# Issuing the expert-row gathers four and four in turn, in place of eight and eight

## The reference

```
for a chunk of 128 tokens, for each of 8 heads:
    s1, i1 = top 16 of the first 128 scores;  s2, i2 = top 16 of the second 128
    cand   = all 256 sums s1 + s2;            top_s, top_c = top 16 of cand
    idx    = 16 expert numbers per token (out of 16384);  gate = softmax(top_s)
    act[k]  = gelu( dot(u_tbl[idx[k]], x) )             k = 0..15
    out    += sum over k of gate[k] * act[k] * v_tbl[idx[k]]
```

## Time and profile before

| | |
|---|---|
| median of 3 runs | 1637.37 us (1636.74 to 1637.39) |
| the profiled execution | 1637.88 us, of which the span is 1636.1 us |
| busy in the span | PE 85%, DVE 61%, POOL 59%, ACT 23% |
| chain that ended last | PE 44%, DMA 26%, issue 10%, DVE 10%, POOL 5%, ACT 4% |
| DMA | 613.88 MB, 375 GB/s over the span; gathers 536.94 MB of it |

### The profile page before, as it was taken

One profiled execution on the slowest core, in us unless ns is written; L12 is line 12 of the kernel. 1 busy time (PEld: TensorE's weight loads), 2 busy tenths in 40 slices (PEclk: granted clock), 3 DMA queues, 4 the chain that ended last, 5 costly groups with the idle time before them and its releaser, 6 DMA issues.

```text
span 1636.1 us, 17816 instructions
## 1 busy us (share of the span) xinstructions
PE 1389.7 (85%) x4977; PEld 802.9 (49%) x4977; DVE 991.3 (61%) x2405; ACT 373.7 (23%) x903; POOL 972.8 (59%) x1038
## 2 busy tenths in 40 slices
PE   7999888887777989876989798986998887888886
PEld 6987454543333554533556455553554553333332
DVE  2147726557677636556656665557774667666664
ACT  1012212212222123322221312232322322222221
POOL 0026545657777655655674755566676477777773
PEclk9999999998998989987999999998999998888887
DMA  9639989999999999999999999999999899999997
GB/s 325 202 115 400 347 309 364 366 363 379 410 410 409 402 394 394 387 395 401 409 404 362 398 394 394 394 396 408 389 409 401 324 410 409 410 409 410 410 409 289
DMA packets 220137, 613.88 MB, mean 375 GB/s; under 512 B 17636, under 2 KB 87332, under 8 KB 220068
## 3 DMA queue, kind: packets, MB, share of 16 engines
q0 software_dynamic: 147456, 536.94, 84.1%
q1 hardware_dynamic: 72468, 75.54, 13.6%
q10 hardware_dynamic: 144, 0.52, 0.1%
HBM read 611.88 MB, written 1.05 MB: 375 GB/s over the span
## 4 chain that ended last, share of the span: by engine, by line
PE 44%; DMA 26%; issue 10%; DVE 10%; POOL 5%; ACT 4%; POOLq 0%; ACTq 0%; DVEq 0%
PE sums L553 28%; DMA rows<-in_peer_u,expert 22%; PE banks L500 11%; DVE rows L1080 4%; POOL rows L455 4%; PE banks L507 2%; POOL rows L467 2%; DMA wring<-in_attn_w_q 2%; DMA wring<-in_w_kv 2%; ACT diag L820 1%; PE sums L507 1%; PE banks L539 1%; ACT L812 1%; DMA rows<-in_peer_v,expert 1%; DVE coef L1098 1%
## 5 line engine op out<-in xcount | busy, mean ns | idle before, releaser
L553 PE MATMUL sums<-rows,diag 128*128 128x512 f32 x2032 | 975.1, 642 | 202.9 <-ACT diag L820 200.1
L1080 DVE SCALAR_TENSOR_TENSOR rows<-rows,xn_near 128x1024 f32<-128x1024 f32 x512 | 616.0, 1220 | 315.5 <-DMA rows<-in_peer_u,expert 305.0
L553 PEld LDWEIGHTS sums<-rows,diag 128*128 128x128 f32 x2032 | 414.2, 207 | 738.9 <-issue 580.6
L467 POOL DMA_INDIRECT rows<-in_peer_v,expert x512 | 483.6, 945 | 342.6 <-PE sums L553 247.9
L455 POOL DMA_INDIRECT rows<-in_peer_u,expert x512 | 487.1, 951 | 299.2 <-issue 249.7
L500 PE MATMUL banks<-xT,wring 128*128 128x128 f32 (+1 forms) x1536 | 210.6, 297 | 7.2 <-DMA wring<-in_attn_w_q 3.3
L500 PEld LDWEIGHTS banks<-xT,wring 128*128 128x128 f32 x1536 | 199.5, 195 | 23.5 <-issue 10.6
L820 ACT ACTIVATE diag<-ident,coef 128x128 f32<-128x128 f32 x508 | 155.5, 388 | 32.0 <-DVE coef L1098 31.8
L812 ACT ACTIVATE gelu<-dots 128x8 f32<-128x8 f32 (+1 forms) x65 | 13.4, 207 | 429.8 <-DVE rows L1080 429.7
L1098 DVE SCALAR_TENSOR_TENSOR coef<-gelu,gate_inv,gate 128x8 f32<-128x8 f32 (+1 forms) x65 | 14.9, 229 | 89.6 <-ACT gelu L812 88.5
L761 ACT ACTIVATE soft<-banks 128x256 f32<-128x256 f32 (+1 forms) x27 | 11.4, 422 | 243.9 <-PE banks L500 243.9
(11 more groups left out here) (115 smaller groups left out, 733.9 us busy)
## 6 DMA issues: line engine op xcount, KB each, us to landing
wring<-in_peer_w_query SPq DMA_DIRECT2D x23, 1024.0 KB, 16.6
wring<-in_w_kv SPq DMA_DIRECT2D x16, 1024.0 KB, 26.0
rows<-in_peer_u,expert POOLq DMA_INDIRECT x512, 10.4
rows<-in_peer_v,expert POOLq DMA_INDIRECT x512, 10.6
wring<-in_attn_w_q SPq DMA_DIRECT2D x8, 1024.0 KB, 23.3
rows<-in_conv_w_in SPq DMA_DIRECT2D x7, 1024.0 KB, 12.0
wring<-in_conv_w_in SPq DMA_DIRECT2D x5, 1024.0 KB, 11.1
wkept<-in_conv_w_out SPq DMA_DIRECT2D x4, 1024.0 KB, 12.0
```

The costliest lines, as they stand in the source:

```text
L467: pool.indirect_dma_start(v_row[j], None, v_table, bass.IndirectOffsetOnAxis(ap=expert[b][:, k:k + 1], axis=0)).then_inc(v_landed[j], 16)
L553: last = nc.tensor.matmul(sums[:, half, :], diag[:, k % GROUP, :], v_row[k % V_SLOTS][:, half * 512:(half + 1) * 512], start=(first and k ...
L1080: nc.vector.scalar_tensor_tensor(out=u_row[j], in0=u_row[j], scalar=1.0, in1=xn_near[:, :, :].rearrange("p a d -> p (a d)"), op0=ALU.mult, ...
```

## The change

For each group the loop over u and the loop over v become two functions, and they are called for the first four places of u, the first four of v, the last four of u and the last four of v. No wait, no semaphore count, no gather and no place changes; only the order in which GpSimd goes through them does. The waits move with their gathers. The other engines' programs stay as they are.

```diff
+            def gather_u(n, b, g, js):
+                for j in js:
+                    if not (isinstance(n, int) and n == 0 and g == 0):
+                        pool.wait_ge(dot_done, GROUP * (GROUPS * n + g - 1) + j + 1)
+                        pool.sem_inc(slot_clear, 1)
+                    elif j % 2 == 0:
+                        early_weights_used(j)
+                    k = g * GROUP + j
+                    pool.indirect_dma_start(
+                        u_row[j], None, u_table,
+                        bass.IndirectOffsetOnAxis(ap=expert[b][:, k:k + 1], axis=0)).then_inc(u_landed[j], 16)
+
+            def gather_v(n, b, g, js):
+                for j in js:
+                    k = g * GROUP + j
+                    if isinstance(n, int) and n == 0 and g == 0:
+                        if k % 2 == 0:
+                            early_weights_used(U_SLOTS + k)
+                    else:
+                        pool.wait_ge(v_used, TOPK * n + k - V_SLOTS + 1)
+                        pool.sem_inc(slot_clear, 1)
+                    pool.indirect_dma_start(
+                        v_row[j], None, v_table,
+                        bass.IndirectOffsetOnAxis(ap=expert[b][:, k:k + 1], axis=0)).then_inc(v_landed[j], 16)
...
                     for g in range(GROUPS):
-                        for j in range(GROUP):
...
-                        for j in range(GROUP):
...
+                        for half in range(2):
+                            first = half * GROUP // 2
+                            gather_u(n, b, g, range(first, first + GROUP // 2))
+                            gather_v(n, b, g, range(first, first + GROUP // 2))
```

## The result

The changed kernel takes 1755.49 us, the median of 4 runs (1754.41 to 1758.8), against 1637.38 for the kernel before (4 runs). The ratio is 1.0721, with an interval of 1.07 to 1.0741: 118 us slower. The profiled execution took 1754.72 us, its span 1753.0, which is 116.9 us more than the span before. In the changed kernel the combine is line 563, the dot products 1090, the coefficients 1108, the gelu 822; the gathers of u are line 450 and those of v line 465.

A forecast was written before the change was run, and what follows sets the result against it. Expert-only stretches were taken as bound by DMA transfers, 20.5 us per group, other stretches differently. Terms 31.4 + 39.3 + 4.8 + 4.4 + 9.9 + 8 - 2.3 = +95.5 us gave 1733 us, range 1660 to 1785.

The forecast's parts named there:

- The loop: Within one group: coefficients, combine rows 0 to 3, v3's issue, u7's issue, landing, dot product, coefficients; 23.8 us against 20.5.
- The last stretch: Expert-only, 1350.04 to 1596.32 us: twelve intervals rise from 246.3 to 285.6 us, +39.3.
- The landing: Time from u7's issue until its rows arrive, with the DMA queue nearly empty once per group: 6.1 us.
- The rival of the short landing: u7 lands in the lowest time seen, 4.2 us; loop 21.9 us, total 1682 us; chance 0.12.
- The clock: Combines in expert-only stretches start at a slow TensorE clock after idling; first matmul to v3's issue takes 10.5 us.
- The rival of the full clock: The combine's first four rows take 7.9 us; loop 21.2 us, total 1668 us; chance 0.08.
- The first expert-only stretch: 350.78 to 531.12 us: one interval of 21.3 us and eight of 23.8, 211.7 against 180.3, +31.4.
- Restarts: GpSimd resumes at 888.36 and 1286.67 us after waiting for experts; u7 is 4.97 us later each time, +9.9.
- The stretch beside attention: 531 to 1332 us: some 24 intervals hide the loop; +8 taken from 0 to +62, plus +4.4 for one interval.
- Up to 350 us: Coefficients wait for ScalarE, which is behind the projection's bank reads, so the new order costs nothing.
- The cover: Up to 350 us, 3.2 us between coefficients being possible at 268.1 and ScalarE letting them go at 271.30.
- The tail: After 1596.32 us: VectorE is done 30.4 us later where it took 32.7 before, -2.3.

The follow-up runs named there:

- six v: Changed kernel with order u0-u3, v0-v5, u4-u7, v6-v7; 2093.24 us, ratio 1.0895, on the chip where the kernel before took 1924.74.
- v first: Changed kernel with order v0-v7, u0-u7; 2498.97 us in one run, on the chip where the kernel before took 1924.74.
- u7 alone: Changed kernel with order u0-u6, v0-v3, u7, v4-v7; 1660.4 us, ratio 1.0126; on the slower chip 1960.19 us, ratio 1.0204.
- two v: Changed kernel with order u0-u3, v0-v1, u4-u7, v2-v7; 1652.82 us, ratio 1.0081; on the slower chip 2037.04 us, ratio 1.0597.
- half the weights: Layer 1's weight blocks load four of eight row tiles: changed kernel 1742.24 us, kernel before 1599.17 us, one run each.
- the ends alone: Kernel before with the new order only in the first two steps and the last group; 1639.49 us against 1638.41, ratio 1.0002.

## Why the prediction was right where it was, and where it missed

- **The loop, 23.8 us.** Right, by its parts: 0.89, 9.94, 4.96, 6.47 and 1.51 us against 0.76, 10.5, 4.97, 6.1 and 1.5. The last stretch has 23.88 on average, +40.3 against +39.3. That the parts and the sum agree this closely is partly luck: the combine's part came 0.6 us shorter than put, the landing and the first step 0.5 longer together. Other orders lengthen or shorten it as its parts say: 27.3 by the sum and 27.37 measured (six v), 35.7 and 36.06 (v first); at 20.1 and 19.9 by the sum the bytes take over, and 20.92 and 20.67 were measured (u7 alone, two v).
- **The landing.** 6.1 was taken; the turn above has 6.4, all gathers a median of 6.5 and a minimum of 4.2. Beside attention the median of u is 8.1 us (565 to 1405), where before it was 14.9 (531 to 1332): inside the 6 to 10 allowed. The estimate of 3.2 us from the Trainium skill ("DMA: Bandwidth & Descriptors", section "Anatomy of one DMA — SWDGE (gpsimd) path") is confirmed in no row. The rival of the short landing (1682) fell with it.
- **The clock.** 10.5 us to v3's issue, measured 9.94: behind 7.77 us of idle the granted clock is 0.50 over the first 4 us of the combine (1525.06 to 1529.06). The rival of the full clock put the loop at 21.2; with the clock held at 1.00 it is 21.65, and 21.49 without the first interval. Its working was right and its condition was not met by the changed kernel on its own.
- **The first expert-only stretch.** +35.0 against +31.4. 2.3 of the 3.6 are the first interval, 23.56 us against the 21.3 put for it; the other eight average 23.98 in place of 23.8. The 21.3 rested on a combine that starts fast after little idle. It had little idle, and started slow. Timeline of TensorE, kernel before, then changed kernel:

```profile
351.67 14.00 PE L553 MATMUL sums<-rows,diag 128*128 128x512 f32 x32 [1.96 <-ACT diag L820]
```

```profile
350.15 15.69 PE L563 MATMUL sums<-rows,diag 128*128 128x512 f32 x32 [1.96 <-ACT diag L830]
```

The granted clock over the first 4 us is 1.00 in the one and 0.67 in the other, after the same 1.96 us of idle, and v3 is issued 9.63 us after the combine's start in place of 7.94: 1.7 of the 2.3.

- **Restarts.** v0 to v3 ahead of u4 to u7 cost their four pitches, and 1.5 us each beyond. GpSimd resumes 10.08 us after the coefficients, as before; u7 follows 13.66 us later, eleven pitches, in place of seven. Timeline of GpSimd, changed kernel:

```profile
934.52 0.94 POOL L450 DMA_INDIRECT rows<-in_peer_u,expert  x1 [12.68 <-DVE expert L1077]
...
948.18 0.94 POOL L450 DMA_INDIRECT rows<-in_peer_u,expert  x1 [0.30 <-issue]
```

From u7's issue to its coefficients (960.44) it is 12.26 us, before it was 10.8 (888.36 and seven pitches, to 907.84). The two restarts cost 6.4 and 6.6 us, 13.0, against 9.9.
- **The stretch beside attention, the term that was mis-sized.** Without the restarts it costs 26.8 us, where 4.4 and 8 were put: over half of the 21 us by which the sum fell short, with the restarts 17.5 of them. The step was the choice inside a range of 0 to 62 by its nearness to a saturated row, and under it the reading that the intervals there are of 24 to 29 us. The coefficients of the kernel before say otherwise. Of 30 intervals from 531 to 1332 without the restarts, ten are no longer than the loop: 15.2, 19.5, 20.4, 20.7, 21.3, 22.3, 23.1, 23.4, 23.4 and 23.8 us. Only the shortest had a term of its own. Timeline of VectorE, kernel before, the shortest, then the same one in the changed kernel:

```profile
1145.05 0.23 DVE L1098 SCALAR_TENSOR_TENSOR coef<-gelu,gate_inv,gate 128x8 f32<-128x8 f32 x1 [5.74 <-ACT gelu L812]
...
1160.25 0.23 DVE L1098 SCALAR_TENSOR_TENSOR coef<-gelu,gate_inv,gate 128x8 f32<-128x8 f32 x1
```

```profile
1198.98 0.23 DVE L1108 SCALAR_TENSOR_TENSOR coef<-gelu,gate_inv,gate 128x8 f32<-128x8 f32 x1 [1.52 <-ACT gelu L822]
...
1222.96 0.23 DVE L1108 SCALAR_TENSOR_TENSOR coef<-gelu,gate_inv,gate 128x8 f32<-128x8 f32 x1
```

Raising each of the ten to a loop of 23.8 us costs 25.0 us, worked out from the kernel before alone; paired with the same intervals of the changed kernel they grew by 24.4 us, 8.8 of it in the one shown (4.4 were put), and the other twenty by 2.4 together. Long landings are the smaller part. Where weights are in flight a turn can be long. One at 646.04, timeline of GpSimd and of VectorE, and the window:

```profile
659.67 0.94 POOL L450 DMA_INDIRECT rows<-in_peer_u,expert  x1 [0.30 <-issue]
...
671.03 1.22 DVE L1090 SCALAR_TENSOR_TENSOR rows<-rows,xn_near 128x1024 f32<-128x1024 f32 x1 [0.28 <-DMA rows<-in_peer_u,expert]
```

```profile
646.00:672.00 26.00, 22.47 (x96) 13.48 (x96) 18.51 (x53) 10.33 (x20) 15.22 (x16) 1.00 1.04 395
```

u7 is 11.36 us under way, above the 6 to 10 that were allowed, and the turn is 26.49 us at a clock of 1.00 and a DMA share of 1.04; 25.3 were put for the bytes, and with a full queue the loop and the bytes can't be told apart. The same interval was 25.17 us before, so it lost 1.3. With half the weights the stretch gives back 14.4 us, of which 0.3 in those ten intervals and the rest in the others: the landing lengthens the long intervals, and the loss beside attention is mostly in the short ones. The pairing is of one profile each, and what a single long interval gains or loses by TensorE's fixed order was not taken apart.
- **Up to 350 us.** Nothing was put and -1.5 measured. The cover, ScalarE behind the projections, held. With the new order in the first two steps alone there was no gain either, and other profiles with the same order there have the coefficients at 349.11 (six spare matmuls), 351.21 (half the weights) and 352.90 (seven), so the 1.5 is not read as a gain.
- **The tail.** -2.0 against -2.3 in one profile. In the kernel with the ends alone it does not show, so that the term came out is not confirmed.

## What to carry to other kernels

Before a wait is moved forward in an in-order queue, write down what is issued behind it and follow that back to what the wait waits for: if it closes a ring within one round of work, the length of the ring replaces the old bound, here 23.8 us for 20.5 and 7.2% of the time, with not a byte or an instruction added. In such a ring latencies count in full (the landing, the pitch of the issues, the cold start of an engine that idles in it), while a loop over two rounds hid them here; two v gathers in place of four ahead of u7 bring it back to 0.8%. A stretch that looks bound by bandwidth can hide such a ring only by the few microseconds between the two, so its intervals are to be priced one by one and not as a whole: here that gives 25.0 us for the ones beside attention, where 12.4 were put and 26.8 measured.

## What the runs showed of the hardware that was not expected

Spare matmuls bought time. With seven of them, and 1.20 to 1.71 us of idle ahead, each of the last eleven of the twelve combines took 14.0 us; with six, a combine after 2.56 us of idle took 13.99 (at 1476.22) and one after only 2.05 us 15.70 (at 1657.95), in the same run: the idle time right ahead does not decide alone. The two combines after 1.96 us, above, say the same.

One chip ran the same kernel 18% slower, 1924.74 us against 1637. No profile of the kernel before was taken there. In the profiles of u7 alone and two v on that chip VectorE stood still inside its own search of the experts, between small steps that need no transfer. Timeline of VectorE, two v on that chip:

```profile
1799.19 0.09 DVE L1046 MATCH_VALUE_LOAD side_i<-side_v,find 128x8 f32 x1 [3.31 <-issue]
...
1801.99 0.43 DVE L1055 TENSOR_TENSOR find<-side_v 128x256 f32<-128x256 f32 x1 [2.44 <-remote]
...
1810.74 0.09 DVE L1046 MATCH_VALUE_LOAD cand_i<-top,find 128x8 f32 x1 [2.39 <-remote]
```

From the coefficients at 1792.38 to the experts' numbers at 1814.00 it took 21.6 us; in six v on the same chip, in a stretch where the DMA share is 0.84, 9.8 us (1830.76 to 1840.57). Why is open. It shows that a ratio between two orders belongs to the chip too: two v is 6.0% slower on that one and 0.8% on the other.
